# First layer: six output blocks begun by quarters of the features instead of four, two pieces behind the last modulation panel

## The reference, cut to what matters

```python
shift, scale, gate = modulation(c, w_mod[layer], b_mod[layer])        # silu(c) @ w_mod + b_mod
shift_c, scale_c, gate_c = modulation(c_ctx, w_mod[layer], b_mod[layer])
h = rms_norm(x, norm_w[layer]) * (1.0 + scale) + shift
hc = rms_norm(xc, norm_w[layer]) * (1.0 + scale_c) + shift_c
proj = h @ w_in[layer]                    # columns: u, v_sgu, za, q, k, v, zb
...
q = apply_axial_rope(rms_norm(split_heads(q, N_Q_HEADS), q_norm_w[layer]), cos, sin)
k, v = kv_heads(k, v, k_norm_w[layer])    # rms_norm of k's heads
k = apply_axial_rope(k, cos, sin)
...
attn = blocked_gqa(q, k_all, v_all)
y = jnp.concatenate([sgu * silu(za), merge_heads(attn) * silu(zb)], axis=-1) @ w_out[layer]
x = x + gate * y
```

## Time and profile before

| | |
|---|---|
| time, median of 3 runs | 3435.49 us (3433.34 to 3438.63) |
| the profiled execution | 3438.4 us, span 3436.3 us |
| PE busy | 3279.5 us, 95% |
| PEld busy | 2911.2 us, 85% |
| DVE busy | 2271.2 us, 66% |
| ACT busy | 1839.8 us, 54% |
| POOL busy | 478.3 us, 14% |
| mean granted clock of TensorE | 0.983 |

### The profile page before, as it was taken

The page is one execution under the profiler, slowest core; times in us unless marked ns, Lnnn a source line. Parts: engine busy times, 40 slices in busy tenths (PEclk is TensorE's granted clock), DMA queues, the critical chain, the costliest instruction groups (busy, mean ns, idle before and its releaser), DMA issues.

```text
span 3436.3 us, 54955 instructions
## 1 busy us (share of the span) xinstructions
PE 3279.5 (95%) x22627; PEld 2911.2 (85%) x22627; DVE 2271.2 (66%) x3089; ACT 1839.8 (54%) x2892; POOL 478.3 (14%) x739
## 2 busy tenths in 40 slices
PE   7999999999999999999999989999989999899997
PEld 3588788787789999999998877888879988799996
DVE  3588889832654556666766576666676555799856
ACT  2344444322566646776775354554546564678644
POOL 0011111111000000000000013777120000322002
PEclk9999999999999999999999999999999999999999
DMA  9755566722234555555554546666554434455454
GB/s 356 262 178 184 184 208 215 287 95 95 92 117 148 178 178 183 190 173 191 179 180 164 174 148 203 200 213 200 176 166 160 141 130 163 149 171 168 157 177 147
DMA packets 174889, 608.44 MB, mean 177 GB/s; under 512 B 21840, under 2 KB 21872, under 8 KB 172848
## 3 DMA queue, kind: packets, MB, share of 16 engines
q1 hardware_dynamic: 145440, 495.54, 42.9%
q0 software_dynamic: 28624, 107.29, 9.2%
q10 hardware_dynamic: 576, 2.10, 0.2%
HBM read 596.27 MB, written 8.57 MB: 176 GB/s over the span
## 4 chain that ended last, share of the span: by engine, by line
PE 75%; DVE 8%; ACT 7%; DMA 7%; issue 3%; SPq 0%; ACTq 0%; DVEq 0%
PE psum_all L584 21%; PE psum_all L580 16%; PE psum_all L582 16%; PE psum_all L577 11%; DMA raw<-in_stream 5%; ACT w_hi L507 2%; DVE w_lo L514 2%; DMA mod_early<-in_stream 1%; DVE xT L873 1%; PE psum_all L1500 1%; PE psum_all L1470 1%; PE psum_all L745 1%; ACT ssd_seg L2228 1%; PE psum_all L3074 1%; DVE ln_d L1076 1%
## 5 line engine op out<-in xcount | busy, mean ns | idle before, releaser
L584 PE MATMUL psum_all<-act_parts,w_lo 128*128 128x256 f32 (+1 forms) x6704 | 2010.7, 300 | 0.0
L514 DVE TENSOR_TENSOR w_lo<-raw,w_hi 128x1024 fp32r<-128x1024 f32 x866 | 1064.1, 1244 | 813.8 <-ACT w_hi L507 812.3
L580 PE MATMUL psum_all<-act_parts,w_hi 128*128 128x256 f32 (+1 forms) x4464 | 1408.2, 315 | 43.5 <-DVE act_parts L972 31.2
L582 PE MATMUL psum_all<-act_parts,w_hi 128*128 128x256 f32 (+1 forms) x4464 | 1378.8, 309 | 0.0
L507 ACT ACTIVATE w_hi<-raw 128x1024 fp32r<-128x1024 f32 x866 | 906.8, 1056 | 800.2 <-DMA raw<-in_stream 798.1
L584 PEld LDWEIGHTS psum_all<-act_parts,w_lo 128*128 128x128 f32 x6704 | 1284.8, 192 | 41.9
L580 PEld LDWEIGHTS psum_all<-act_parts,w_hi 128*128 128x128 f32 x4464 | 857.9, 192 | 116.1 <-issue 53.8
L582 PEld LDWEIGHTS psum_all<-act_parts,w_hi 128*128 128x128 f32 x4464 | 858.4, 192 | 42.9 <-issue 3.4
L577 PE MATMUL psum_all<-act_parts,w_hi 128*128 128x512 f32 x2240 | 804.8, 403 | 29.8 <-DVE w_lo L514 15.7
L577 PEld LDWEIGHTS psum_all<-act_parts,w_hi 128*128 128x128 f32 x2240 | 424.9, 190 | 139.5 <-issue 26.3
L873 DVE SCALAR_TENSOR_TENSOR xT<-mod_late,small,xT 128x1024 f32<-128x1024 f32 x210 | 256.6, 1279 | 8.9 <-DMA mod_late<-in_stream 6.7
(11 more groups left out here) (491 smaller groups left out, 3396.3 us busy)
## 6 DMA issues: line engine op xcount, KB each, us to landing
raw<-in_stream SPq DMA_DIRECT2D x858, 512.0 KB, 3.3
mod_late<-in_stream POOLq DMA_DIRECT2D x128, 512.0 KB, 4.6
mod_early<-in_stream SPq DMA_DIRECT2D x128, 256.0 KB, 6.4
ssd_seg<-acs_rows POOLq DMA_DIRECT2D x8, 1536.0 KB, 6.8
s_matrices<-s5p_made POOLq DMA_DIRECT2D x16, 384.0 KB, 4.3
raw<-in_stream SPq DMA_DIRECT2D x16, 256.0 KB, 5.4
s_made<-s_matrices POOLq DMA_DIRECT2D x16, 256.0 KB, 3.0
xT<-in_x SPq DMA_DIRECT2D x1, 2048.0 KB, 10.3
```

The source lines that it names most:

```text
L514: dve.tensor_tensor(w_lo[:, n % RING, :], raw[:, n % RING, :], w_hi[:, n % RING, :].bitcast(F32), ALU.subtract).then_inc(lo_ready, 1)
L580: pe.matmul(sums, w_hi[:, n % RING, cols], block.rhs(kk, HIGH, block.width), start=(kk == 0), stop=False)
L582: pe.matmul(sums, w_hi[:, n % RING, cols], block.rhs(kk, LOW, block.width), start=False, stop=False)
L584: last = pe.matmul(sums, w_lo[:, n % RING, cols], block.rhs(kk, HIGH, block.width), start=False, stop=(kk == block.kt - 1))
```

## The change

`QUARTERED` becomes 6: q0 and zb0 are begun by quarters too. Each panel is followed by three lead units, each a quarter of two blocks; there are 12 lead units for 8, and 854 whole ones for 858. In panels 2 and 3 TensorE has six pieces (k = 4 to 14); in panel 4 the last two are taken out of the panel and stand behind its turn (`HELD_BEHIND`). The products of six blocks fill banks 0 to 5, so the turned panels go to the panel's own bank (6 or 7, for 5), the first unit of a panel waits for `mod_added`, and k's sums and turns go to banks 0 and 1. q's first sum also waits for zb0 taken out of its bank. The late operations begin at unit 9 and spread over 75 units, for 6 and 78.

```diff
-QUARTERED = 4
+QUARTERED = 6
...
+HELD_BEHIND = ((3, 12), (3, 14))
...
-LATE_SLOTS = 78
-LATE_FROM = 6
+LATE_SLOTS = 75
+LATE_FROM = 9
...
             if k == 0 and q >= 2:
-                pe.wait_ge(mod_rows_ready, q - 1)
+                pe.wait_ge(mod_added, q - 1)
...
-                last = pe.matmul(psum[5][:, 4 * b:4 * b + 4], rows[panel % len(rows)][:, b * P:(b + 1) * P],
+                last = pe.matmul(psum[6 + panel % 2][:, 4 * b:4 * b + 4], rows[panel % len(rows)][:, b * P:(b + 1) * P],
...
-                    if q and k in range(4, 4 + 2 * QUARTERED, 2):
+                    if q and k in range(4, 4 + 2 * QUARTERED, 2) and (q, k) not in HELD_BEHIND:
                         piece(QUARTERED * (q - 1) + (k - 4) // 2)
                 mod_turn(pe, early_rows, 3)
+                piece(3 * QUARTERED - 2)
+                piece(3 * QUARTERED - 1)
...
-                    split_to(2 * q + 1)
+                    split_to(QUARTERED // 2 * q + 1)
...
-                    split_to(2 * q + 2)
+                    split_to(QUARTERED // 2 * (q + 1))
...
-                p_bank, s_bank = (2, 3), 2
+                p_bank, s_bank, k_banks = (2, 3), 2, (psum[0], psum[1])
...
                 if h == 0:
                     pe.wait_ge(k_roped.sem, k_roped.at(N_KV))
+                    pe.wait_ge(taken["act"], blocks[at["zb", 0]].count)
...
-                    half = slice(n // 2 % 2 * 512, n // 2 % 2 * 512 + 512)
+                    half = slice(n // (QUARTERED // 2) % 2 * 512, n // (QUARTERED // 2) % 2 * 512 + 512)
```

More of the change, by code:

```diff
@@ L772, in early_modulate @@
                          for x in (modulation[:, 0:4 * KT], param("b_mod", 0, 4 * KT)))
-            sums = psum[5][:, 0:16].rearrange("p (b h v) -> p b h v", h=2, v=2)
+            sums = psum[6 + q % 2][:, 0:16].rearrange("p (b h v) -> p b h v", h=2, v=2)
             dve.tensor_tensor(out, sums, bias, ALU.add).then_inc(mod_added, 1)
@@ L1405, in layer_flow @@
                 y_hi, y_lo = (a[:, KT * T:2 * KT * T].rearrange("p (k t) -> p k t", t=T) for a in (act_hi, act_lo))
-                p_bank, s_bank = (6, 7), 4
+                p_bank, s_bank, k_banks = (6, 7), 4, (psum[4], psum[5])
             else:
                 y_hi, y_lo = (a[:, :].rearrange("p (k t) -> p k t", t=TT) for a in (act_hi, act_lo))
-                p_bank, s_bank = (2, 3), 2
+                p_bank, s_bank, k_banks = (2, 3), 2, (psum[0], psum[1])
             H, G = N_Q, SGU_GROUPS
@@ L1431, in k_sum @@
                     pe.wait_ge(k_rooted.sem, k_rooted.at(j))
-                pe.matmul(psum[4], const("over_128"), sq[:, :], start=True, stop=True).then_inc(k_stats.sem, 1)
+                pe.matmul(k_banks[0], const("over_128"), sq[:, :], start=True, stop=True).then_inc(k_stats.sem, 1)
             def k_turn(pe, j):
@@ L1437, in k_turn @@
                     pe.wait_ge(k_roped.sem, k_roped.at(j))
-                pe.matmul(psum[5][:, 0:T], const("rotate"), k[:, j, 0:T], start=True, stop=True).then_inc(k_spun.sem, 1)
+                pe.matmul(k_banks[1][:, 0:T], const("rotate"), k[:, j, 0:T], start=True, stop=True).then_inc(k_spun.sem, 1)
             def turn_v(pe, j):
@@ L1591, in scalar_early @@
                         act.wait_ge(k_normed.sem, k_normed.at(j))
-                    act.activation(root[:, :], psum[4], ACT.Sqrt, bias=const("eps_rms")).then_inc(k_rooted.sem, 1)
+                    act.activation(root[:, :], k_banks[0], ACT.Sqrt, bias=const("eps_rms")).then_inc(k_rooted.sem, 1)
                 if g in at_slot.v_copy:
@@ L1655, in k_scale, with turn_forth @@
                                          in1=root[:, :], op0=ALU.mult, op1=ALU.mult).then_inc(k_normed.sem, 1)
-            def turn_forth(dve, x):
+            def turn_forth(dve, x, bank):
                 ordered = order["vector"]
-                dve.tensor_tensor(spin[:, :], psum[5][:, 0:T], const("sin"), ALU.mult)
+                dve.tensor_tensor(spin[:, :], bank[:, 0:T], const("sin"), ALU.mult)
                 dve.tensor_tensor(x, x, const("cos"), ALU.mult).then_inc(ordered.sem, 1)
@@ L1666, in k_rope @@
                 dve.wait_ge(k_spun.sem, k_spun.at(j + 1))
-                turn_forth(dve, k[:, j, 0:T]).then_inc(k_roped.sem, 1)
+                turn_forth(dve, k[:, j, 0:T], k_banks[1]).then_inc(k_roped.sem, 1)
                 dve.wait_ge(k_roped.sem, k_roped.at(j + 1))
@@ L1676, in q_rope @@
                 dve.tensor_scalar(s[:, 0:chunks], s[:, 20:20 + chunks], P ** -0.5, None, ALU.mult)
-                turn_forth(dve, q[:, h % 2, 0:T]).then_inc(q_roped.sem, 1)
+                turn_forth(dve, q[:, h % 2, 0:T], psum[5]).then_inc(q_roped.sem, 1)
                 dve.wait_ge(q_roped.sem, q_roped.at(h + 1))
```

## The result

| | changed | before, same chips | ratio, 95% interval |
|---|---|---|---|
| median | 3452.5 us (3444.8 to 3454.3, 6 runs) | 3434.2 us (3427.5 to 3438.6, 6 runs) | 1.0042 (1.0029 to 1.0056) |
| the same kernel in a later comparison | 3452.6 us (6 runs) | 3437.8 us (25 runs) | 1.0033 (1.0020 to 1.0046) |
| the profiled execution | 3454.3 us, span 3452.2 | 3438.4 us, span 3436.3 | +15.9 us |

A forecast was written before the change was run, and what follows sets the result against it. TensorE, busy 95% of the span, bounds the kernel, with the opening narrowly held by DMA. Terms 8.1 - 1.0 - 0.3 + 2.5 = +9.3 gave a median of 3444.8 us, range 3434 to 3452 (the forecast's own 3440 to 3450).

The forecast's parts named there:

- The opening, +8.1: To the end of the last modulation unit: four more pieces and a lead unit, less vanished waits, cost 8.1 us.
- The lead unit's +1.3: Ahead of the second panel: one more lead unit's 0.52 MB load at 403 GB/s costs 1.3 us.
- Rival (c): Panels of the opening: the third lead unit starves them of loads, with a clock fall; +4, 3449 us; chance 0.10.
- To the heads, -1.0: From the last modulation unit to q1: the filled 3.16 us wait slightly outweighs two new waits; 1.0 us gained.
- 7.2 us for k0's rotation: At the turn of k1: TensorE waits 7.2 us while VectorE's chain finishes rotating k0.
- 3.9 for zb0: At q0's sum, sharing a bank with zb0: TensorE waits 3.9 us for ScalarE to apply Silu.
- The charge of 1.8 us: Behind each of the two new waits: TensorE's clock at half rate slows nine matmuls, costing 1.8 us each.
- The end of layer 0, +2.5 (0 to 4.5): Near 652 us: `w_lo` comes late behind more late adds; a wait and part of a clock fall cost 2.5 us.
- units 80 and 81 get seven adds, not six: End of layer 0: with the new late numbers the extra adds make the next `w_lo` 2.4 us later.
- 0 if loads of `mod_late` hide it: End of layer 0: lower bound of that cost, nothing if waiting loads cover the extra adds.
- Rival (a): At the heads: work pulled forward pays in full, k0's rotation and zb0 being ready in time; 3427 us; chance 0.14.
- Rival (b): VectorE's chain exposed, but no clock fall behind the waits and no late `w_lo`; +3.2, 3438.7 us; chance 0.16.

The follow-up runs named there:

- late12_bank3: Changed kernel with LATE_FROM 12, LATE_SLOTS 72, and q0's turn and sums in bank 3; ratios to before 1.0039 and, run again, 1.0014.
- q0_turn_bank3: Changed kernel with layer 0's turn and sums of q0 in bank 3, so they need not wait for zb0 taken; 3452.4 us, ratio 1.0041.
- none_held: Changed kernel with all six pieces inside the fourth panel and none behind its turn; ratio to before 1.0055.
- late_from_12: Changed kernel with LATE_FROM 12 and LATE_SLOTS 72, so no late adds ahead of k's chain on VectorE; 3451.7 us, ratio 1.0043.
- late_by_loads: Changed kernel with the last two panels' late operations counted 1.5 times when spread over units; ratio to before 1.0037, run again 1.0021.
- held_on_before: Kernel before with only the hold: the fourth panel's last two of four pieces stand behind its turn; 3432.3 us, ratio 0.9982.

## Why the prediction was right, and where its sizes were off

**The opening, +8.1: +9.5.** The lead unit's +1.3 was 1.27; so close an agreement is luck, since the second panel starts between 46.1 and 48.0 in the nine traces with this opening. The rest was short by small sums: the turn in panel 3 came 4.9 us later than before (81.56 for 76.64), where the terms gave 4.4; panel 4 another 4.2 (111.34 for 102.18 is 9.2 in all), where they gave 3.7; and 0.4 more within the last panel. The miss is no larger than the spread of this stage: in the same nine traces the last turn starts between 132.7 and 135.2, and it started at 125.4 and 124.0 in the two of the four blocks without the hold. Rival (c)'s waits were small where they came at all: 0.56 and 0.45 us for `mod_early` in panel 4, in late12_bank3 and q0_turn_bank3.

**To the heads, -1.0: -0.4.** The mechanism was right in every step: the 3.16 us wait filled (none_held shows it back), 7.2 us for k0's rotation (7.00), 3.9 for zb0 (3.76). Both causes are shown: late_from_12 took 3.9 us from the one, q0_turn_bank3 2.5 from the other with its clock fall. q1 began 45.6 us behind the last unit (179.82) where the terms gave 44.5; the 1.1 us are about what q0's turn and sums lost at half clock (2.55 us for 1.24 before). The charge of 1.8 us for the clock behind each wait stands for something that is not fixed, and in this trace it was 1.1 us too small for the two together: behind the first wait, from the turn of k1 to the end of zb0's quarter it took 5.5 us (168.03 to 173.51) and 3.4 in late12_bank3 at full clock, so 2.1; behind the second 14.9 us to the scores (177.27 to 192.18) for 12.3 before, so 2.6. Both falls came in both traces of the changed kernel, but the second need not come: behind a wait for Silu of the same length the clock stayed full in none_held and in late_by_loads, again.

**The end of layer 0, +2.5 (0 to 4.5): +7.7.** This is the term that was mis-sized. Its place was right (`w_lo` late behind adds, past 628 us), its reason was the smaller part: "units 80 and 81 get seven adds, not six". The seven adds stand there, but from the first to the split behind them it took 14.1 us (650.96 to 665.08) for 9.8 of six adds before (640.60 to 650.44), and one add is 1.2 of these 4.3 us. The waits for loads among them grew from 1.8 to 5.0. I took waiting loads for something that would hide the cost ("0 if loads of `mod_late` hide it"); they made the larger part of it. The last two panels need one load for each operation, and the adds wait for those loads (11.0 us in all, 6.7 before, 1.6 and 3.2 with fewer loads a unit). Of the 7.7 us the late numbers alone made 3.7 in one trace; the other 4.0 came with six blocks in both traces of the changed kernel (79.4 and 79.0), while q0_turn_bank3 and none_held, with the same numbers, took 76.2 and 75.4. Why is open: the order of work there is the same, and only when the loads fall differs. That alone can move this stage: held_on_before, with the old numbers and k0's sum 4.8 us sooner, took 74.2 for 71.7, and late12_bank3 took 77.5 and 79.3 in its two traces. My theory that the first 79.4 us were a bad draw fell with the second trace of the changed kernel; how far this opening fixes the size is not shown by two traces.

**Sum.** +9.3 forecast; +15.9 in the profiled execution, +14.4 and +11.3 by the two ratios. The direction and its mechanism stood: the opening's cost is not earned back at the heads. The size of the whole was met only in part, since the term of the end of layer 0 was 5.2 us short and most of the other misses added to it. Rival (a), the work pays in full, needed both waits gone. late12_bank3 left 3.12 and 1.26 us of them; its two traces have the first scores 1.7 us ahead of the kernel before and 1.3 behind (181.37 and 184.39 for 183.05), and the end of layer 0 puts both behind (4.3 and 9.9 us at the last late turn). The 9.5 us of the opening come back only as far as the heads run without a wait. Rival (b) fell by the clock falls and the end of the layer; rival (c) by the missing waits for `mod_early` at panels 3 and 4 of the changed kernel, though the wait ahead of panel 2 grew by 1.8 us (4.12 for 2.31).

## What to carry to other kernels

Work pulled forward into a stage that TensorE already fills is only moved; what pays is the part of it that lands in a wait, here two pieces of 2.85 us behind one turn, and that part needed none of the rest. When blocks are taken out from between two steps of a chain on another engine, add up that chain in the order in which its engine runs it, bystanders included: here four adds of a different computation made 3.9 of 7 us. And spread background work by its scarcer resource: operations were even over the units, loads were not, and the units with a load for each operation were where TensorE waited. The edit that spread them by loads thinned the adds there too, so how much of its gain is due to each was not tested.

## What was unexpected of the hardware

The same wait does not always cost the same. In two executions of one kernel TensorE stood still 3.12 us at the same instruction; in one the granted clock stayed 1.00, in the other it was 0.50 until 168 us and fell again to 0.57 behind 172, and the way from k0's sum to the first scores was 4.3 us longer. The Trainium skill (TensorE: Matmul & The Clock Gate, Part 1) has an idle array clocked at half rate until it has been busy again, and lets the place of the change vary from run to run. One of the two executions agrees with the first half; the other, at 1.00 through the same pause, shows that a pause of this length can also pass without the fall. The 3.75 us wait for Silu shows it too: the matmul behind it took 1.19 us in late_by_loads and 0.67 in the second execution of it. The wait of 7.0 us was always paid for: all six traces that have it show 1.19 us behind it.

The two executions of each of these pairs ran on different chips, so the chip could be the cause. A wait for `w_lo` in a later layer, which all 14 traces have at 3.5 to 3.6 us, tells otherwise. On one chip it cost the clock in none_held and not in late12_bank3:

```profile
2103.24 0.77 PE L579 MATMUL psum_all<-act_parts,w_hi 128*128 128x512 f32 x1 [3.56 <-DVE w_lo L516]
...
2083.25 0.47 PE L579 MATMUL psum_all<-act_parts,w_hi 128*128 128x512 f32 x1 [3.55 <-DVE w_lo L516]
```

The first row is of none_held, the second of late12_bank3. Ten of the 14 traces have the 0.47 us and four have 0.76 or 0.77; two chips show both.

The spread between executions of one kernel goes with the clock: for late_by_loads spans of 3450.4 and 3434.9 us had mean granted clocks of 0.980 and 0.984. At half rate for 0.8% more of the span, TensorE does 0.4% of the span less, which is 14 us, an estimate from these two clocks. How much of the spread between executions is due to the clock was not tested by itself.
